# Stick-breaking attention: masks, softplus and the output projection's halves in other places

## The reference, cut to what matters

```python
hn = rmsnorm(h, a_norm_g[i])
qkv = (hn @ a_w_qkv[i]).reshape(B, T, 3, SB_HEADS, SB_HEAD_DIM)
o = stick_breaking_attention(q, k, v)
h = h + merge_heads(o) @ a_w_o[i]
h = h + squared_relu_mlp(h, mlp_norm_g[layer], ...)

# stick_breaking_attention, for one block of queries
z = jnp.einsum('bhqd,bhkd->bhqk', qb, kf) * scale
past = key_pos[None, :] < q_pos[:, None]
log_keep = jnp.where(past, jax.nn.log_sigmoid(-z), 0.0)
after = lax.cumsum(log_keep, axis=3, reverse=True) - log_keep
w = jnp.where(past, jnp.exp(jax.nn.log_sigmoid(z) + after), 0.0)
o = jnp.einsum('bhqk,bhkd->bhqd', w, v)
```

## Time and profile before

| what | value |
|---|---|
| median of three runs | 3012.33 us (3006.33 to 3018.25) |
| the profiled execution | 3014.8 us |
| its span in the trace | 3013.0 us |
| PE busy | 2699.6 us (90%) |
| DVE busy | 1171.9 us (39%) |
| ACT busy | 1007.9 us (33%) |
| POOL busy | 862.7 us (29%) |
| mean granted TensorE clock | 0.952 of full speed |

### The profile page before, as it was taken

How to read it: one execution, slowest core, us unless ns; L and a number is a source line. 1 busy time by engine, 2 the same in 40 slices (tenths; PEclk the granted TensorE clock), 3 DMA queues, 4 the chain that set the end, 5 groups by cost and what they waited for, 6 DMA issues and landing times.

```text
span 3013.0 us, 42132 instructions
## 1 busy us (share of the span) xinstructions
PE 2699.6 (90%) x16870; PEld 2198.5 (73%) x16870; DVE 1171.9 (39%) x2087; ACT 1007.9 (33%) x2020; POOL 862.7 (29%) x604
## 2 busy tenths in 40 slices
PE   4999899999989888888888879999988888999998
PEld 3887677777866545555777759999987777777777
DVE  4753555432232121111345572224445555612112
ACT  3334344333232211112334344322233444532331
POOL 0001354322330122200222214655531001265553
PEclk7989999999999999999899989999998888999999
DMA  3322011233334999997211102323321111123331
GB/s 100 91 52 63 15 36 29 70 98 84 100 121 183 426 426 426 427 421 296 64 43 50 43 15 84 95 82 91 99 64 49 36 36 37 51 82 92 104 91 64
DMA packets 316036, 364.15 MB, mean 121 GB/s; under 512 B 14128, under 2 KB 289584, under 8 KB 291264
## 3 DMA queue, kind: packets, MB, share of 16 engines
q1 hardware_dynamic: 315840, 361.42, 34.3%
HBM read 359.29 MB, written 2.10 MB: 120 GB/s over the span
## 4 chain that ended last, share of the span: by engine, by line
PE 71%; DVE 8%; DMA 7%; ACT 6%; POOL 4%; issue 3%; DVEq 0%; ACTq 0%; SPq 0%; POOLq 0%
DMA early<-in_w_up_e 7%; PE bank L1703 6%; PE bank L2164 5%; PE bank L2165 5%; PE bank L2166 5%; PE bank L443 5%; PE bank L444 5%; PE bank L445 5%; PE bank L2595 4%; PE bank L2596 4%; PE bank L2597 4%; POOL split L2141 2%; PE bank L1001 1%; PE bank L1727 1%; PE bank L1003 1%
## 5 line engine op out<-in xcount | busy, mean ns | idle before, releaser
L2141 POOL TENSOR_TENSOR split<-keep,split 128x1024 fp32r<-128x1024 f32 x144 | 352.3, 2451 | 351.6 <-ACT split L2115 351.6
L2164 PE MATMUL bank<-x_hi,split 128*128 128x264 f32 (+1 forms) x1280 | 404.2, 316 | 19.9 <-POOL split L2141 8.1
L2165 PE MATMUL bank<-x_lo,split 128*128 128x264 f32 (+1 forms) x1280 | 397.9, 311 | 0.0
L2166 PE MATMUL bank<-x_hi,split 128*128 128x264 f32 (+1 forms) x1280 | 396.5, 310 | 0.0
L1703 PE MATMUL bank<-early 128*64 128x256 f32 x2048 | 237.6, 387 | 47.1 <-DVE early L1803 18.8
L2164 PEld LDWEIGHTS bank<-x_hi,split 128*128 128x128 f32 x1280 | 247.6, 193 | 43.4 <-issue 22.7
L2115 ACT ACTIVATE split<-keep 128x1024 fp32r<-128x1024 f32 x192 | 200.5, 1051 | 227.1 <-PE bank L2597 210.8
L1703 PEld LDWEIGHTS bank<-early 128*64 128x64 f32 x2048 | 171.8, 139 | 126.1 <-issue 52.8
L2165 PEld LDWEIGHTS bank<-x_lo,split 128*128 128x128 f32 x1280 | 247.5, 193 | 10.7 <-issue 0.5
L2166 PEld LDWEIGHTS bank<-x_hi,split 128*128 128x128 f32 x1280 | 246.5, 193 | 11.0
L443 PE MATMUL bank<-x_hi,w_split 128*128 128x512 f32 x416 | 170.0, 409 | 15.7 <-DVE w_split L431 15.7
(11 more groups left out here) (459 smaller groups left out, 6161.2 us busy)
## 6 DMA issues: line engine op xcount, KB each, us to landing
early<-in_w_gate_e SPq DMA_DIRECT2D x64, 1024.0 KB, 10.8
early<-in_w_up_e SPq DMA_DIRECT2D x64, 1024.0 KB, 10.9
early<-in_w_down_e SPq DMA_DIRECT2D x64, 1024.0 KB, 11.1
early<-in_w_in SPq DMA_DIRECT2D x66, 512.0 KB, 3.7
keep<-in_mlp_w_in SPq DMA_DIRECT2D x64, 512.0 KB, 3.9
keep<-in_mlp_w_out SPq DMA_DIRECT2D x64, 512.0 KB, 4.0
keep<-in_a_w_qkv SPq DMA_DIRECT2D x24, 512.0 KB, 3.7
early<-in_w_ssd_out SPq DMA_DIRECT2D x16, 512.0 KB, 3.9
```

Of the source, the lines that this page charges most:

```text
L2141: e.tensor_tensor(lo, x, whole(hi), ALU.subtract).then_inc(*u.free(sig_, "lo", n))
L2164: e.matmul(o, hi[:, k, :], XH2[:, k, n0:n1], start=k == 0, stop=False, skip_group_check=True)
L2165: e.matmul(o, hi[:, k, :], XL2[:, k, n0:n1], start=False, stop=False, skip_group_check=True)
L2166: m = e.matmul(o, lo[:, k, :], XH2[:, k, n0:n1], start=False, stop=k == 7, skip_group_check=True)
```

## The change

It has seven parts.

1. **Join.** Squares of the norm are made earlier on ACT, one after each `hi`; piece 1 of the weights is split by DVE, in the join; `sums_pe` comes after the second product instead of the first.
2. **Softplus.** ACT takes |z| straight from PSUM, then exp(-|z|) and ln(1 + x); DVE's "keep" is max(z, 0) plus that. DVE's min with 40 is gone.
3. **Masks.** Two constant tiles `IDENTA` and `NEGA` are written by ACT at the start of the join; after the scores PE adds a matmul of the two on each masked square (-1e30 where the key is not past). POOL's two selects for each unit are gone, and DVE and PE wait for DVE and ACT instead.
4. **Turned weights.** For t = 1 and 2 both heads' turned tiles share one bank and one exp.
5. **Feeds.** In the attention the split feeds always go to `+ 3` (before: `+ 2` for j < 4).
6. **Output projection.** Its eight weight pieces are halves in k (4 x 256 columns). `("first", i)` does the product over heads 0 to 7 (k = 0 to 3) in eight of the last twelve steps, and DVE adds it into `R`; `("second", 0)` does k = 4, 5 of the products 0 and 1 at step 37; `outa_*` does the rest.
7. **Layout.** In layer 1's MLP the split activations lie as tiles of 512 instead of 528 columns.

```diff
         def combine_act(e):
             e.wait_ge(*F.pe.to("oT", 31, 1))
             table(e, SET_EXP_LN)
+            e.wait_ge(*B.act.now())
+            for y, x, scale in ((IDENTA, C["ident"], 1.0), (NEGA, C["upto"], NEG)):
+                e.activation(y, x, ACT.Copy, scale=scale).then_inc(*SA.act.up("mask"))
             for what, q, s_ in COMBINE:
                 if what == "turn":
...
                     if q and 2 <= s_ < 6:
                         NA1.hi(e, s_ - 2)
+                    if q and s_ >= 6:
+                        NA1.square(e, s_ - 6)
+            split_hi(e, 2)
+            for t in range(2, 4):
+                NA1.square(e, t)
             for t in range(4, 8):
                 NA1.hi(e, t)
-            for t in range(8):
                 NA1.square(e, t)
...
-        plan += [(wao2, 0, 8, c, 128, None) for c in COLS8]
+        plan += [(wao2, k0, 4, 256 * c, 256, None) for k0 in (0, 4) for c in range(4)]
...
-            return plan[n][5] is not None or AT_WAO <= n < AT_MLP[0] or plan[n][2] == 4
+            return n == 1 or plan[n][5] is not None or AT_WAO <= n < AT_MLP[0] or plan[n][2] == 4
...
+        PARTSA = (27, 29, 30, 31, 32, 34, 35, 36)
         ATTA = [("lin", (0, j)) for j in range(9)]
         for step in range(39):
             ATTA += [(f, step - lag) for f, lag in (("z", 0), ("sv", 3)) if 0 <= step - lag < 36]
             if step < 27:
                 ATTA.append(("lin", (step // 9 + 1, step % 9)))
+            if step in PARTSA:
+                ATTA.append(("first", PARTSA.index(step)))
             if step in (12, 21, 30):
                 ATTA.append(("split", step // 9 - 1))
             if 0 <= step - 2 < 36:
                 ATTA.append(("t", step - 2))
+            if step == 37:
+                ATTA.append(("second", 0))
         ATTA.append(("split", 3))
...
+        def turned_heads(t):
+
+            return [] if t == 0 else [[0, 1]] if t < 3 else [[0], [1]]
+
...
+        def outa_product(e, bs, i, ks):
+
+            k0 = ks.start // 4 * 4
+            x, hi, lo = split_parts(AT_WAO + k0 + i // 2)
+            c = cols(i % 2, 128)
+            for k in ks:
+                e.wait_ge(*(OA.dve if k % 2 else OA.pool).to("lo", k))
+                for b, (n0, n1) in zip(bs, HALVES2):
+                    o, yh, yl = b.ap[:, 0:n1 - n0], OSH[:, k, n0:n1], OSL[:, k, n0:n1]
+                    e.matmul(o, hi[:, k - k0, c], yh, start=k == k0, stop=False, skip_group_check=True)
+                    e.matmul(o, hi[:, k - k0, c], yl, start=False, stop=False, skip_group_check=True)
+                    m = e.matmul(o, lo[:, k - k0, c], yh, start=False, stop=k == k0 + 3, skip_group_check=True)
+            return m
+
...
+                if what == "first":
+                    bs = [BR.take("fa", i, h) for h in range(2)]
+                    for b in bs:
+                        for s, v in b.before:
+                            e.wait_ge(s, v)
+                    e.wait_ge(*split_done(AT_WAO + i // 2))
+                    outa_product(e, bs, i, range(0, 4)).then_inc(*WS.of(AT_WAO + i // 2).free(OA.pe, "first", i))
+                if what == "second":
+                    for j in range(2):
+                        bs = [XR.take("oa", j, h) for h in range(2)]
+                        for b in bs:
+                            for s, v in b.before:
+                                e.wait_ge(s, v)
+                        e.wait_ge(*split_done(AT_WAO + 4))
+                        outa_product(e, bs, j, range(4, 6))
                 if what == "lin":
                     p, j = i
                     n = atta_weights(p, j)
...
-                        if p == j == 0:
+                        if p == 0 and j == 1:
...
+                        two = scored(i)[j - 1:j + 1] if j % 2 and t < 4 else scored(i)[1:3] if j == 3 else []
+                        for _, _, zb, zc in two:
+                            m = e.matmul(zb.ap[0:r, zc.stop - r:zc.stop], IDENTA[0:r, 0:r], NEGA[0:r, 0:r], start=False, stop=True,
+                                         skip_group_check=True)
...
-                    for a in range(2 if t else 0):
-                        b = BR.take("wT", i, a)
+                    for heads in turned_heads(t):
+                        b = BR.take("wT", i, heads[0])
                         for s, v in b.before:
                             e.wait_ge(s, v)
-                        for k in range(1, t + 1):
-                            m = e.transpose(b.ap[:, cols(k - 1, 128)], x[:, a, slice(*TILESA[k])], C["ident"])
-                        m.then_inc(*SA.pe.up("wT", i, a))
+                        for a in heads:
...
-                    e.wait_ge(*SA.pool.to("w", i))
+                    e.wait_ge(*SA.act.to("w", i))
...
-                    split_hi(e, atta_weights(p, j) + (2 if j < 4 else 3))
+                    split_hi(e, atta_weights(p, j) + 3)
...
-                    x = lanes(i)
-                    e.wait_ge(*SA.dve.to("low", i))
-                    e.activation(x, x, ACT.Exp).then_inc(*SA.act.up())
+                    u, x = EB.take(i), lanes(i)
+                    for s, v in u.before:
+                        e.wait_ge(s, v)
+                    e.wait_ge(*SA.pe.to("z", i))
+                    if STICK[i][1] == 4:
+                        e.wait_ge(*SA.dve.to("copied", i))
+                    for a, ks, z in read(i):
+                        e.activation(x[:, a, ks], z, ACT.Abs).then_inc(*SA.act.up())
+                    e.wait_ge(*SA.act.now())
+                    e.activation(x, x, ACT.Exp, scale=-1.0).then_inc(*SA.act.up())
                     e.wait_ge(*SA.act.now())
...
-            e.wait_ge(*SA.pool.to("keep", i))
+            e.wait_ge(*SA.dve.to("keep", i))
...
+                if what == "first":
+                    split_lo(e, AT_WAO + i // 2 + 3, True)
+                    e.wait_ge(*OA.pe.to("first", i))
+                    for h, (n0, n1) in enumerate(HALVES2):
+                        b, r = BR.of("fa", i, h), R[:, i, n0:n1]
+                        e.tensor_tensor(r, r, b.ap[:, 0:n1 - n0], ALU.add).then_inc(*b.free(OA.dve, "first", i))
...
-                    split_lo(e, atta_weights(p, j) + (2 if j < 4 else 3), True)
+                    split_lo(e, atta_weights(p, j) + 3, True)
...
-                    u = EB.take(i)
                     x = lanes(i)
-                    for s, v in u.before:
-                        e.wait_ge(s, v)
                     e.wait_ge(*SA.pe.to("z", i))
                     if STICK[i][1] == 4:
                         b = BR.of("zm", i)
-                        e.tensor_copy(ZM.take(i).ap, b.ap[:, 0:32]).then_inc(*b.free(SA.dve))
-                        e.wait_ge(*SA.dve.now())
-                    for a, ks, z in read(i):
-                        y = x[:, a, ks]
-                        e.tensor_scalar(y, z, 40.0, None, ALU.min).then_inc(*SA.dve.up("low", i))
+                        e.tensor_copy(ZM.take(i).ap, b.ap[:, 0:32]).then_inc(*b.free(SA.dve, "copied", i))
                     if i > 0:
                         stick_sums(e, i - 1)
                     e.wait_ge(*SA.act.to("soft", i))
                     for a, ks, z in read(i):
                         y = x[:, a, ks]
-                        e.tensor_tensor(y, y, z, ALU.max).then_inc(*SA.dve.up("keep", i))
+                        e.scalar_tensor_tensor(out=y, in0=z, scalar=0.0, in1=y, op0=ALU.max, op1=ALU.add).then_inc(*SA.dve.up("keep", i))
                     if i == 35:
...
-                    split_lo(e, atta_weights(*i) + (2 if i[1] < 4 else 3), False)
-                if what == "z":
-                    hs, t, qs, n = stick(i)
-                    y, r = lanes(i)[:, :, qs], qs.stop - qs.start
-                    e.wait_ge(*SA.dve.to("keep", i))
-                    e.affine_select(out=y, in_=y, compare_op=ALU.is_gt, fill=0.0, base=0, pattern=[[0, len(hs)], [-1, r]],
-                                    channel_multiplier=1).then_inc(*SA.pool.up("keep", i))
-                if what == "t":
-                    hs, t, qs, n = stick(i)
-                    real_, meta = weights_of(i)
-                    y, r = meta if t == 0 else real_[:, :, cols(t - 1, 128)], qs.stop - qs.start
-                    e.wait_ge(*SA.act.to("w", i))
-                    e.affine_select(out=y, in_=y, compare_op=ALU.is_gt, fill=0.0, base=0, pattern=[[0, len(hs)], [1, r]],
-                                    channel_multiplier=-1).then_inc(*SA.pool.up("w", i))
...
         def outa_pe(e):
-            for i, n in WAO:
-                linear_pe(e, OA, n, ("oa", i), HALVES2, (lambda k: [(OA.dve if k % 2 else OA.pool).to("lo", k)]) if i == 0 else None, (OSH, OSL))
+            for i in range(8):
+                n = AT_WAO + 4 + i // 2
+                if i < 2:
+                    m = outa_product(e, outa_banks(i), i, range(6, 8))
+                else:
+                    bs = [BR.take("oa", i, h) for h in range(2)]
```

(16 more changed lines are left out.)

69 lines of the change are left out of this document (42 added, 27 removed).

## The result

| | before | after |
|---|---|---|
| median | 3014.53 us (3006.33 to 3018.25, 4 runs) | 2972.26 us (2969.93 to 2974.27, 4 runs) |
| ratio, 95% interval | | 0.9864 [0.9845, 0.9883] |
| span of the profiled execution | 3013.0 us | 2970.4 us |
| mean granted clock | 0.952 | 0.960 |

A forecast was written before the change was run, and what follows sets the result against it. PE was taken as fullest but waiting, with one unit's chain setting the pace at the norm's sums and late steps. Terms 0.8 - 8 - 24.1 - 2.8 = -34.1 us gave 2980.7 from 3014.8, 2978 on the median; range 2955 to 2996.

The forecast's parts named there:

- Layer 1's stride: Layer 1's MLP: tiles of 512 instead of 528 columns bring nothing (same matmuls, same columns).
- First nine products: Products before the steps: second product no longer waits for the norm's sums; -8 us, bounds 3 and 12.
- Steps with a product: The 27 steps with a product: waits and half clock go, masks and late DVE add; -24.1 us, bounds -30 and -16.
- The masks: Steps with a product: two added mask matmuls per unit, 0.27 us a pair, 27 steps; +7.3 us.
- The half clock: Steps with a product: slow 1.2 GHz matmuls after each wait for v's split go, 24 matmuls three times; -6.5 us.
- (a): Steps with a product: PE's three waits for DVE's split of v's second half of weights go; -19.8 us.
- (c): Steps with a product: sv's 13 waits for POOL's second select go, since ACT releases PE itself; -7.5 us.
- Last twelve steps and projection: End of attention: projection matmuls move into the steps but wait for banks behind DVE's adds; -2.8 us, bounds -17 and +12.
- rival 1: Last twelve steps fill as in layer 1: -17 us for steps and projection, 2964 us in all; chance 0.25.
- rival 2: Last twelve steps' chain runs at the half clock: +12 instead of -3 us, 2993 us in all; chance 0.12.
- rival 3: Feed brings nothing: split of v's second half waits for a ring slot or ACT; 3004 us; chance 0.06.
- rival 4: ACT's |z|, exp and ln pace the 27 steps, so slower: 3046 us at 2.5 us a step; chance 0.04.

The follow-up runs named there:

- e1: Kernel before with part 7 alone (layer 1's split activations as tiles 512 columns apart): ratio 0.9988.
- e2: Kernel before with layer 1's MLP tiles still 528 columns apart, their data moved 16 columns earlier to each tile's start: ratio 1.0001.
- e2b: Kernel before with part 7 and every tile moved on by 16 columns (64 bytes): ratio 0.9993.
- e9: Kernel before with layer 1's tile data at multiples of 128 bytes, 544 and 512 columns apart in turn: ratio 0.9983.
- e3: Kernel before with part 5 alone (feeds always three pieces ahead): 3006.54 us, ratio 0.9975.
- e5: Kernel after without part 6, the output projection whole and behind the last step: 2972.45 us.
- e7: Kernel after with the last unit's scans and logs on DVE moved behind the adds of first half-product number 6: 2962.56 us.
- e8: e7's kernel with k = 4, 5 of projection products 2 and 3 ahead of the last parts of 0 and 1: 2961.56 us.
- e4_join: Kernel before with part 1 alone (earlier squares, piece 1 split by DVE, norm's sums after the second product): 3014.18 us, ratio 1.0002.

## Why the prediction was right

**The whole.** 2978 forecast, 2972 measured; -34 us forecast, -42 measured, of which 7 are a term that was put at nothing. By stretch the forecast was within 2 us everywhere but in two places: layer 1's MLP (-6.8, forecast nothing) and the stages ahead of the change (-2.1, which also move from one profile to the next: the join's start lay between 1411 and 1420 in all kernels).

**Layer 1's stride "at nothing" failed.** The step's reason was "same matmuls, same columns", and the earlier trace rows's row of layer 1 was read for its count, not for its pace. A matmul of 512 columns starts every 0.232 us there, with nothing that it waits for; the placements of e1, e2, e2b and e9 show that where its operands lie sets part of this.

**First nine products: right, -9.7 for -8.** The second product's parts came as told: contention of the `lo` (0.75 us of wait) and of the split (1.35), 2.1 for the 3 that were taken, and 3.0 for the banks behind the roots, for about 4. DVE and POOL side by side there (L2211 is the last `lo`, L2221 POOL's last add, L2149 the splits):

```profile
1461.00 1.83 DVE L2211 SCALAR_TENSOR_TENSOR x_lo<-lasting,x_hi 128x528 fp32r<-128x528 f32 x1
1462.40 1.60 POOL L2221 TENSOR_TENSOR squares_a<-squares_a 128x528 f32<-128x528 f32 x1
1462.75 2.33 DVE L2149 TENSOR_TENSOR split<-keep,split 128x1024 fp32r<-128x1024 f32 x1
1463.96 3.36 POOL L2149 TENSOR_TENSOR split<-keep,split 128x1024 fp32r<-128x1024 f32 x1
```

The `lo` ends 0.4 us after POOL's add ahead of 1462.40 is over, though it began at 1461.00 (0.76 us alone). DVE's split ends 1.1 us after POOL's last add (1.22 alone), and POOL's split 2.2 us after DVE's (2.34 to 2.38 in the kernel before, against 3.36 here). Within what POOL's rough spans can tell, each of them makes no progress, but for some 0.1 to 0.3 us of it, while an instruction of the other engine that began earlier is running. The Trainium skill's rule ("SBUF — State Buffer", the entry on the shared port pair), that one of the two engines fully blocks, agrees with these rows. What is lost is the rest of the instruction that is running, not a whole one: the first two `lo` lost 0.28 and 0.48, the third some 0.5, the last 1.07 and the split 1.11, in all 3.4 us. The forecast's reading by the rule took a whole add for each of the five, 7 us, and so came to -4; its reading by a mean of 1.54, about 4, was near in size, but that mean is one of such rests and no milder form of contention (one of its eight took 2.30 us, from 2626.02 to 0.6 us past the end of the POOL split that the earlier trace rows shows).

**Steps with a product: the sum right (-22.5 for -24.1), the terms not separable.** The waits for the split (-19.8) and for POOL (-7.5) both went, and what remains after them in the trace is 2.0 for the logs (forecast 2.4, three times). The masks cost more than forecast: a pair of 128 columns holds PE for 0.37 us (1577.19 to 1577.56), so 24 x 0.37 and six pairs of 16 at 0.14 make 9.7, not 7.3. The half clock: the steps' -22.5 less these parts (-19.8 - 7.5 + 9.7, and +1.1 for the other waits, 7.8 now against 6.7 before) leaves -6.0, for -6.5; it is what is left over, not a measurement. But the forecast priced (a) and (c) as if each stood by itself, and the rival "the feed brings nothing" as 26 us. e3 shows that the feed alone brings 5: its wait turns into one for POOL. (c) was called worth 7.5; with the feeds in place it is 12.3 net of the masks. Each row of waits was true only while the longer wait ahead of it held PE.

**Last twelve steps and projection: right, -1.8 for -2.8**, and so is the mechanism: banks behind DVE's adds. The sizes are less so: 0.7 for 2.2 at step 27, 1.8 for 1.8 before the scores of step 31, 1.2 for 4.1 in step 32, 1.5 for 4 before sv, 4.4 for 6 at step 36, 2.5 for 2.4 at the end. That is 12.6 us of waits in the stretch, for 20.5. The last twelve steps nevertheless took 80.5 (75 to 85 forecast): PE's own work was 67.9 us at clock 0.87, which at full clock is some 59, for the 57.8 of the sum. Two errors cancel here, the waits too long by 8 and the clock too high, worth 10 less the 2 that were added for it. That part of the hit is luck. The projection took 26.3 for 20 to 24 and the norm. e5 confirms that part 6 as written brings next to nothing, and e7 that DVE's order costs 4 us of it.

**Rivals.** The tail does not fill as in layer 1 (rival 1), though this stretch is 9.2 us shorter in e7 and 12.2 in e8 than in the kernel before, of the 17 us (3 of them in steps that neither edit touches). It does not run at half clock (rival 2). The feeds do what they are there for (rival 3): the waits for DVE's split are gone from the steps. ACT does not pace the steps (rival 4): the largest wait for it there is 0.5 us.

## What to carry to other kernels

A wait of 20 us in a list is not a gain of 20 us: ask what the same engine would have waited for next, in the same places, and change both together (feeds 5, the rest 0.5, together 22.5). Work that frees a bank stands in an in-order queue; look at what is ahead of it (moving one unit's scans behind two adds was worth 4 us in its place, twice what moving half a projection brought). And read the pace of back-to-back matmuls with no waits in it before and after any change of a tile's pitch.

## What was not expected of the hardware

- Where operands lie in SBUF changes the pace of 512-column matmuls by 2%: 0.2319 us from start to start with tiles 528 columns apart, 0.2274 with tiles 512 apart that start at multiples of 128 bytes, 0.2301 if those start 64 bytes off, 0.2308 at 544 and 512 in turn. What in the hardware does this was not found. The Trainium skill ("TensorE: Matmul & The Clock Gate", "Wait — 56ns, not 53.3ns?") gives 215.7 ns for this size; no placement here reached it.
- The clock of a stretch whose code is not changed differs between profiles: the last twelve steps of the kernel before at 0.76 (56.3 us), 0.66 (59.9, e4_join) and here, in e2_start, 0.63:

```profile
1731.80:1793.00 61.20, 44.99 (x295) 28.64 (x295) 41.54 (x101) 27.95 (x62) 9.49 (x22) 0.63 0.00 1
```
- A scan on DVE over two times 528 keys took 2.41 us in the kernel after and 4.47 in e3_feed, where POOL's split had begun 0.3 us ahead of it. Its end at 1632.19 is 2.4 us after that split's at 1629.76: it did its work only then, as in the first products.
